# Compressed scores dealt out in two groups, a later place for one step's products, an earlier weight split: a hybrid decoder step on one core

## What is computed

```python
ck, cv = compress(k_cmp, pe[0], w[0]), compress(v_cmp, pe[1], w[1])   # 32-row blocks, stride 16
p_cmp = softmax(mask(q @ ck))                  # compressed branch: 31 blocks per prompt row
p_slc = softmax(mask(q_rot @ k_sel))           # selected blocks
p_win = softmax(mask(q_rot @ k_win))           # window
o = g0 * p_cmp @ cv + g1 * p_slc @ v_sel + g2 * p_win @ v_win
y = o @ w_out1
```

## Time and profile before

| what | value |
|---|---|
| median of 3 runs | 1343.24 us (1341.97 to 1344.81) |
| the profiled execution's own time | 1342.97 us |
| its span in the trace | 1341.2 us |
| PE / POOL / DVE / ACT busy, share of the span | 96% / 60% / 54% / 48% |
| attention head, prompt steps, samples | about 708 to 747, 747 to 889, 889 to 923 us |
| output projection of layer 1, then the next block | about 923 to 966, 966 us on |

### The profile page before, as it was taken

The page is one execution under the profiler, slowest core; times in us unless marked ns, Lnnn a source line. Parts: engine busy times, 40 slices in busy tenths (PEclk is TensorE's granted clock), DMA queues, the critical chain, the costliest instruction groups (busy, mean ns, idle before and its releaser), DMA issues. The chain is left out here.

```text
span 1341.2 us, 27440 instructions
## 1 busy us (share of the span) xinstructions
PE 1284.5 (96%) x10530; PEld 1193.9 (89%) x10530; DVE 721.1 (54%) x1213; ACT 644.7 (48%) x1160; POOL 808.9 (60%) x703
## 2 busy tenths in 40 slices
PE   6999999999999999999998998989999999999997
PEld 6999998999999999999986555657989999999997
DVE  5448587776776222211755767654877767761112
ACT  5412466666665233311313566653666666652332
POOL 7435447888888666644311554442578888886662
PEclk9999999999999999999999999999999999999999
DMA  5322223334333233337864042031233343333331
GB/s 182 95 95 69 91 64 95 95 110 112 95 95 97 87 86 88 115 96 167 195 143 89 18 139 66 1 87 32 64 95 96 105 116 96 95 97 87 87 102 68
DMA packets 211067, 127.87 MB, mean 95 GB/s; under 512 B 31868, under 2 KB 206004, under 8 KB 210958
## 3 DMA queue, kind: packets, MB, share of 16 engines
q1 hardware_dynamic: 210958, 126.40, 34.1%
HBM read 117.82 MB, written 5.38 MB: 92 GB/s over the span
## 5 line engine op out<-in xcount | busy, mean ns | idle before, releaser
L2177 POOL TENSOR_TENSOR WL<-WR,WH 128x512 fp32r<-128x512 f32 x236 | 317.6, 1377 | 274.6 <-ACT WH L537 274.6
L477 PE MATMUL PG<-G,WH 128*128 128x260 f32 x1856 | 298.9, 283 | 3.5 <-POOL WL L2177 3.5
L477 PEld LDWEIGHTS PG<-G,WH 128*128 128x128 f32 x1856 | 253.2, 188 | 6.3 <-POOL WL L2177 5.8
L537 ACT ACTIVATE WH<-WR 128x2048 fp32r<-128x2048 f32 x59 | 112.9, 1914 | 284.8 <-PE PG L477 249.2
L477 PE MATMUL PG<-H,WH 128*128 128x260 f32 x1312 | 216.6, 287 | 4.3 <-DVE H L2398 2.3
L852 PE MATMUL M<-HB,WH 128*128 128x260 f32 x1056 | 202.9, 290 | 8.4 <-POOL WL L714 4.9
L477 PE MATMUL PG<-G,WL 128*128 128x260 f32 x928 | 186.8, 282 | 0.0
L477 PEld LDWEIGHTS PG<-H,WH 128*128 128x128 f32 x1312 | 180.5, 190 | 6.4 <-POOL WL L2177 2.3
L714 POOL TENSOR_TENSOR WL<-WR,WH 128x512 fp32r<-128x512 f32 x132 | 169.5, 1297 | 21.1 <-ACT WH L706 21.1
L852 PEld LDWEIGHTS M<-HB,WH 128*128 128x128 f32 x1056 | 164.1, 190 | 18.1 <-POOL WL L714 15.6
L1323 POOL TENSOR_SCALAR PB<-PB,ST,GT 128x512 f32<-128x512 f32 (+3 forms) x128 | 80.1, 635 | 130.9 <-DVE ST L1776 130.4
(11 more groups left out here) (289 smaller groups left out, 2451.6 us busy)
## 6 DMA issues: line engine op xcount, KB each, us to landing
WR<-in_w_ffn_in SPq DMA_DIRECT2D x88, 512.0 KB, 4.9
WR<-in_w_in SPq DMA_DIRECT2D x32, 512.0 KB, 4.6
WR<-in_w_ffn_out SPq DMA_DIRECT2D x32, 384.0 KB, 4.1
WR<-in_w_ffn_out SPq DMA_DIRECT2D x32, 320.0 KB, 3.4
WR<-in_w_in SPq DMA_DIRECT2D x18, 256.0 KB, 4.4
WR<-in_w_out SPq DMA_DIRECT2D x8, 512.0 KB, 4.0
PST<-in_cache_kv SPq DMA_DIRECT2D x32, 128.0 KB, 2.3
WR<-in_w_out SPq DMA_DIRECT2D x16, 256.0 KB, 5.1
```

What stands on the lines that cost most here:

```text
L477: mm = pe.matmul(PG[:, par, hf, 0:HALF], w, x, start=(first and at_k == 0 and n == 0), stop=(last and at_k == nk - 1 and n == 2))
L537: w_hi.on(act.activation(WH[:, b, :], WR[:, b, :], ACT.Copy))
L2177: low = pool.tensor_tensor(WL[:, b, c:c + 512], WR[:, b, c:c + 512], WH[:, b, c:c + 512].bitcast(F32), ALU.subtract)
```

## The change

Five edits. Of the compressed scores, PE makes group 0 (16 scores) by place 5, the scores of step 1 at places 6 and 7, `x` = 16 at place 9 and the rest at places 10 to 14. DVE takes group 1 out (`cmp_in(1)`) after the maxima of step 1 and `cmp_norm(0)`. In PE's round for step 1 the products of step 0, with their wait for `CVK`, stand behind the turns of step 1 and the scores of step 3. ACT splits `out1`'s slot 1 after the last sample probabilities, where it waits for `ss_done` = 3; `act_out_blocks` leaves that split out for layer 1.

```diff
@@ -749,7 +749,7 @@  act_out_blocks
-                if m in (0, 2, 4):
+                if m in (0, 2, 4)[l:]:
                     split_next_wide(act, name, m // 4, m % 4 // 2)
@@ -1456,14 +1456,15 @@  pe_attention
-            def some_scores():
-                for x in todo[0:3]:
+            def some_scores(n=3):
+                for x in todo[0:n]:
                     cmp_score(x)
-                del todo[0:3]
+                del todo[0:n]
             for jj in range(2):
                 scores(0, jj)
             some_scores()
-            compress(pe, 1, {**{l: some_scores for l in range(1, 11)}, 12: lambda: scores(1, 0), 14: lambda: scores(1, 1)})
+            compress(pe, 1, {**{l: some_scores for l in (1, 2, 3, 4, 10, 11, 12, 13, 14)}, 5: lambda: some_scores(1),
+                             6: lambda: scores(1, 0), 7: lambda: scores(1, 1), 9: lambda: some_scores(1)})
@@ -1520,15 +1521,19 @@  pe_attention, the loop over the steps
-                if hu == 1:
-                    q_wait_drained(pe, Q_CV)
-                for q, kt in late[-1:] * (hu > 0 and FIRST[hu - 1]) + late[0:len(late) - (hu > 0 and FIRST[hu - 1])]:
-                    pv(hu - 1, q, kt)
+                def products():
+                    for q, kt in late[-1:] * (hu > 0 and FIRST[hu - 1]) + late[0:len(late) - (hu > 0 and FIRST[hu - 1])]:
+                        pv(hu - 1, q, kt)
+                if hu != 1:
+                    products()
                 for jj in range(2):
                     for q, kt in part(now, jj):
                         turn(hu, q, kt)
                     if hu + 2 < len(STEPS):
                         scores(hu + 2, jj)
+                if hu == 1:
+                    q_wait_drained(pe, Q_CV)
+                    products()
                 if hu == 0:
                     turn_cv()
@@ -1802,10 +1807,10 @@  dve_attention
             cmp_max(0)
-            cmp_in(1)
             for jj in range(2):
                 row_max(1, jj)
             cmp_norm(0)
+            cmp_in(1)
             drain_ck(1)
@@ -2036,6 +2041,7 @@  act_attention, the samples
             exp_s(2)
             drain_p(act, 1, 2)
+            split_hi(act, (S0["out1"] + 1) % 2, raw_of("out1", 1), (ss_done, 3))
             drain_os(act, 1)
```

## The result

The changed kernel takes 1335.18 us (median of 4 runs, 1333.50 to 1336.67), the kernel before 1342.92 us beside it (4 runs, 1341.97 to 1344.81): ratio 0.994, 95% interval 0.9923 to 0.9958. That is 7.7 us between the medians, where 6.2 were forecast. The profiled execution took 1335.96 us, its span is 1334.2 us.

What follows compares the result with a forecast made beforehand. PE's work was taken to bound the prompt steps (busy 129 of 138 us), so its waits in the head and output projection count. From 1342.97 us profiled, 5.1 (head) and 1.1 (split) gave 1336.8, median 1337.0 us; range 1335.0 to 1339.8.

Steps and rivals of the forecast that it cites:

- First turn: Head, PE's first turn: 1.1 us sooner, with 0.2 us of new wait ahead of PE's loop.
- The third stop: Step 0, PE waiting for DVE to empty a bank: 0.7 us left instead of 2.85, last prompt turn 3.4 us sooner.
- The clock behind it: Scores behind the 2.85 us stop in step 0: the clock's fall goes, 1.5 us gained, bounds 0 and 1.6.
- Rival A: Step 0: the clock falls all the same, as PE still stops twice; 1338.5 us, chance 0.17.
- The products: Step 0's products behind step 1's turns: the 0.20 us stop goes, 0.2 us gained; bounds gain 0.2, loss 0.4.
- The steps: Prompt steps, PE busy 129 of 138 us: what is won ahead reaches the samples undiminished.
- Rival C: Prompt steps: another engine paces them and absorbs the head's gain; 1342.1 us, no difference, chance 0.07.
- D: Steps 0 to 2: the low clock stays at 1.2 GHz after the first stop; 1346 us, slower, chance 0.04.
- The split: Output projection, second slot split earlier: tile 0's DVE chain no longer stretched by POOL, 1.1 us; bounds 0 and 1.48.
- Rival B: Output projection: part 3's loss returns at the next slot, tile 1 held or DVE slowed; 1338.1 us, chance 0.17.
- The side effect taken at 0: Samples' end: POOL's split beside DVE's closing chain may stretch it; 0 taken, 1.1 us as the bound.
- the median of the runs lies 0.27 above the profiled one: Last step of the sum: 0.27 us between profiled execution and median, taking 1336.8 to 1337.0 us.

Runs made afterwards that it cites:

- split-alone kernel: The kernel before with only the two edits that move ACT's split of out1's second slot earlier; ratio 0.9999 (0.9976 to 1.0023).
- first stop filled: The kernel before with two unused products ahead of the 17th compressed score, keeping PE busy through its 1.42 us stop; ratio 0.9988 (0.9970 to 1.0007).
- the repeat: The changed kernel run again with nothing edited; 1335.57 us (6 runs), ratio to the kernel before 0.9941.
- head-alone kernel: The changed kernel with the second slot's split put back in its old place, only the head's edits left; 1334.86 us, ratio 0.9937.
- the old dealing: The changed kernel with PE's old dealing of the scores, keeping DVE's new order; 1349.35 us.
- the 2.85 us stop filled: The kernel before with five unused 512-column products ahead of the last prompt turn of step 0; 1347.68 us.
- the first run with POOL kept busy: The changed kernel with six unused POOL subtractions, starting when ACT has the samples' high parts; 1336.44 us.

## Why the prediction fell short

The direction was right, and the mechanisms that it counted on are in the trace; the gain was put too small, and the forecast of 1337.0 us lies above the medians of all timed kernels that have both the new head and the new split (1334.27 to 1335.57).

- *First turn*, a part of the next term. 1.1 us forecast, 1.30 measured; the new wait is 0.25, forecast 0.2.
- *The third stop.* 3.4 us forecast, 3.74 measured, since 0.40 us of it are left and not 0.7. DVE empties the bank nearly 0.4 us sooner than worked out. About 0.1 of this is the compression, which ends at S + 18.84 and not 18.96. About 0.2 is a gap between its end and ACT's shift that the prediction carried over from the kernel before (727.1 to 727.4): there ACT was in the exponentials of step 1 until 728.75, now it has been idle for 3.82 us and starts 0.07 us after the end.
- *The clock behind it.* 1.5 us forecast, 5.30 - 3.74 = 1.56 measured. But this is the difference to the very execution that the prediction had read, and the price is not the same in each. The same piece of PE's program behind the same stop took 3.70 us in the kernel before, 3.34 in the split-alone kernel and 2.82 in the one with its first stop filled (in this order below, columns as in the earlier trace rows; the clock is the third number from the end):

```profile
734.17:737.87 3.70, 3.70 (x16) 2.17 (x17) 1.84 (x3) 0.59 (x1) 1.07 (x3) 0.55 0.00 0
```

```profile
733.47:736.81 3.34, 3.34 (x16) 1.65 (x17) 1.74 (x3) 0.59 (x1) 1.09 (x3) 0.61 0.03 5
```

```profile
733.59:736.41 2.82, 2.82 (x16) 1.45 (x17) 1.74 (x3) 0.59 (x1) 1.08 (x3) 0.74 0.02 6
```

  The first turn of step 2 came at S + 38.88, 38.52 and 37.99 there, so against these executions the head gains 5.55, 5.19 and 4.66 us. That the term came out to 0.06 us is luck of the execution that was read; that the piece's length goes with the clock is shown. With PE kept busy through the stop the same piece took 2.09 us. Rival A, the fall all the same in the changed kernel, is not seen in its profiles. (The row cited for the clock after the 1.39 us stop covers the stop itself; the windows behind it, 740 to 750, are at 1.00 too.)
- *The products.* 0.2 forecast, 0.25 measured by undoing them alone.
- *The steps.* 174.98 against 175.06 us: what was won ahead comes through. Rival C falls, and D, the low clock staying, is not seen in the changed kernel.
- *The split.* 1.1 forecast, 1.06 measured, alone and with the rest. The place is shown, the size is partly luck: the prediction priced one subtraction (1.50 to 0.43 us), but the one ahead of it also lost 0.50 us, and DVE then waits for ACT's `HB`, which takes about as much back. Rival B did not happen here, but happened when the split was moved once more. The side effect taken at 0 is there (1.24 against 0.28 us) and hidden, as argued.

These terms sum to 6.6 us against 6.2. **The step that failed** in the sum is its last one, "the median of the runs lies 0.27 above the profiled one". That offset belongs to three executions and not to the kernel: in the result the median lies 0.78 us below the profiled execution, in the repeat 0.55 below, in the head-alone kernel 0.88 above. Why one execution lies above its median and another below is not shown. Of the 1.8 us between the forecast and 1335.18 this step makes 1.05; the terms make 0.4, nearly all of it the third stop, put at 3.4 and measured at 3.74; the last 0.4 lies in stretches that no edit touches (0.46 ahead of S, 0.08 in the steps, -0.15 at the end), put at nothing. The range's lower bound does not follow from its own working either: 1337.0 less 0.4 (1.48 for 1.1) and 1.3 is 1335.3 and not 1335.0.

**What failed in the mechanism** is the price of the first stop. The prediction took "the 1.42 us go" as the whole of it, from one execution whose clock behind this stop was 1.00. Rival A's question, does a stop bring the fall, was asked only of the changed kernel and not of the kernel before. There the answer is: in some executions. Two profiles show a fall behind this same stop, 5.0 us in the one where it can be read alone. It lasted about 10 us with PE at work, where the prediction had held against rival D that the fall stayed under 4.6. None of the four runs beside the result is long (to 1344.81 us); in the longer comparisons the kernel before has medians of 1343.75 and 1343.72, so that the repeat gained 8.2 us where its stages give 6.6. Of those 35 runs the 21 up to 1345 us have a median of 1342.59 us, and the 14 others reach 1352.25; the 30 runs of the five kernels with several runs in which the stop is replaced by the scores of step 1 lie between 1332.88 and 1338.68. The mean granted clock of each run sides with this: ten of the 14 have 0.984 to 0.989, of the 21 only one, of the 30 none below 0.990.

What stays open: the share of executions with the fall, and whether it explains all of the long ones. Four of the 14 (to 1346.07 us) and the one long run of the kernel with its first stop filled (1347.00) have a clock of 0.992 or 0.993, as short runs have. The mean clock is a rough sign, since it counts falls anywhere in a run: the profile with the fall of 5.0 us has 0.992, and so has the changed kernel's, whose clock was down from 10 to 30 us (0.73 and 0.76) and never in the head. The two groups of the split-alone kernel are 8 us apart, and the kernel with the first stop filled has fewer long executions but a time that can't be told from that of before.

## What to carry to other kernels

A stop of TensorE ahead of a long stretch of dense products is not priced by its length alone: read the granted clock behind it in several executions, and fill the stop with work that is due anyway. When one group of work is dealt sooner to fill a stop, the engine that empties its results must be reordered with it; here the order of VectorE alone put a stop of 4.46 us ahead of the loop, and the dealing without it (with the later products) gained 0.3 us. In this kernel a GpSimd pass over SBUF cost nothing where VectorE worked from PSUM or waited; moved beside a chain that others wait for, it only carried the wait one slot on. And a price that hangs on the clock is one execution's: it was 1.56, 1.20 and 0.68 us behind one stop here.

## What the runs showed of the hardware

The same stop of 1.42 us, in the same program up to there, was followed by the full 2.4 GHz in the profiles of the kernel before and of the split alone, and by some 10 us at 1.2 GHz, with PE busy throughout, in two others (the old dealing, and the 2.85 us stop filled). The stop of 2.85 us, where it was not filled, was followed by a fall each time, to 0.55, 0.61 and 0.74 over the same piece. After the stops of 1.39 us for `CVK` no fall was seen. The Trainium skill (TensorE: Matmul & The Clock Gate, What's actually happening) says that the watch over the engine's activity runs freely and not from the kernel's start; by that the same stop can have either outcome, and these traces agree, though no run here shows the watch itself.

VectorE beside GpSimd's subtractions of two SBUF operands: 0.43 to 1.52 us for 128x260, 0.28 to 1.24 for 128x64, and 0.71 to 5.07 for eight of 128x8, the most in proportion for the smallest (tile 0, the samples' end, and the first run with POOL kept busy). The addition with an operand in PSUM stayed at 0.69 us. The Trainium skill (GPSIMD Engine Reference, Key points) says that the two engines share their SBUF interfaces; the traces agree, and the sizes are those of the runs.
